# Early dot products of a product-key expert layer: from 64, 32 and 32 beside three stages to 96, 32 and none

## The reference, cut to what matters

```python
gates   = sigmoid(gate_logits + b_gate)            # gate_logits = x @ w_in[:, gate columns]
widened = einsum('bsgw,gwd->bsgd', branches, w_branch)
mix     = sum_g(gates * widened) @ w_out
h       = LN(ALPHA * x + mix)
# PEER, for blocks of 128 tokens; it, gt: 128 expert numbers and gates of each token
q    = h @ w_peer_q                                # scores, top-k -> it, gt
act  = gelu(einsum('td,ted->te', xt, u_tab[it]))   # 128 dot products of length 1024 per token
out  = einsum('te,ted->td', gt * act, v_tab[it])
```

## Time and profile before

| | |
|---|---|
| time of three runs, median | 4244.49 us (4243.42 to 4244.56) |
| the profiled execution's own time | 4240.24 us |
| its span, first to last instruction | 4238.4 us |
| busy share of PE, DVE, ACT, POOL | 87%, 64%, 32%, 37% |
| HBM traffic over the span | 267 GB/s |

### The profile page before, as it was taken

How to read it: one execution, slowest core, us unless ns; L and a number is a source line. 1 busy time by engine, 2 the same in 40 slices (tenths; PEclk the granted TensorE clock), 3 DMA queues, 4 the chain that set the end, 5 groups by cost and what they waited for, 6 DMA issues and landing times.

```text
span 4238.4 us, 46211 instructions
## 1 busy us (share of the span) xinstructions
PE 3702.3 (87%) x14431; PEld 2456.2 (58%) x14431; DVE 2717.4 (64%) x5493; ACT 1369.5 (32%) x2741; POOL 1555.7 (37%) x1317
## 2 busy tenths in 40 slices
PE   7999989799888798586437889799799999999998
PEld 5777867678777677475114445354354544545763
DVE  1444443316776766649799988988886867842550
ACT  1444443233434433126024042150240413314540
POOL 2555534230000177465455344443454544520000
PEclk8999999899999899897769999899899999999999
DMA  7667623355444377688989999999999999973557
GB/s 242 198 202 228 205 68 93 94 178 163 139 135 146 88 240 245 228 303 302 374 333 408 383 375 376 347 404 368 354 400 398 406 403 387 395 307 128 184 196 271
DMA packets 505249, 1133.37 MB, mean 267 GB/s; under 512 B 37932, under 2 KB 250076, under 8 KB 504832
## 3 DMA queue, kind: packets, MB, share of 16 engines
q1 hardware_dynamic: 336512, 570.42, 39.1%
q0 software_dynamic: 147456, 536.94, 33.3%
q10 hardware_dynamic: 21120, 24.12, 1.6%
HBM read 1044.28 MB, written 89.41 MB: 267 GB/s over the span
## 4 chain that ended last, share of the span: by engine, by line
PE 33%; DVE 14%; DMA 5%; issue 2%; ACT 1%; POOL 0%; DVEq 0%; ACTq 0%
PE ps L1262 26%; DVE u_ring L2209 6%; DMA u_ring<-in_peer_u,pidx 4%; PE ps L1248 4%; PE ps L1295 2%; DMA v_ring<-in_peer_v 1%; DVE split_v L2259 1%; ACT split_v L1673 1%; DVE hot L2201 1%; DVE hot L2202 1%; PE h_up L1237 0%; DVE pick_own L1847 0%; DVE pick_own L1852 0%; DVE got_own L1855 0%; DVE inds_own L1798 0%
## 5 line engine op out<-in xcount | busy, mean ns | idle before, releaser
L1262 PE MATMUL ps<-v_ring,table 128*128 128x512 f32 x3584 | 1594.3, 596 | 21.3 <-DMA v_ring<-in_peer_v 20.0
L895 POOL DMA_INDIRECT u_ring<-in_peer_u,pidx x896 | 862.6, 963 | 1011.5 <-DVE coefe L2209 940.3
L2209 DVE CUSTOM_DVE_ANT_0 u_ring<-u_ring,h_up 128x1024 f32<-128x1024 f32 x896 | 1060.1, 1217 | 157.9 <-DMA u_ring<-in_peer_u,pidx 148.2
L1262 PEld LDWEIGHTS ps<-v_ring,table 128*128 128x128 f32 x3584 | 664.3, 191 | 778.7 <-issue 725.2
L844 POOL TENSOR_TENSOR w_lo<-w_raw,w_hi 128x1024 fp32r<-128x1024 f32 x200 | 443.7, 2224 | 881.2 <-ACT w_hi L1368 875.9
L954 PE MATMUL ps<-x_hi,w_hi 128*128 128x512 f32 x1280 | 521.7, 408 | 61.5 <-ACT w_hi L1368 52.8
L957 PE MATMUL ps<-x_lo,w_hi 128*128 128x512 f32 x1280 | 508.4, 397 | 0.0
L1248 PEld LDWEIGHTS ps<-hot,hot 128*128 128x128 f32 x2048 | 282.5, 204 | 184.9 <-issue 103.6
L1641 ACT ACTIVATE table<-ps 128x512 f32<-128x512 f32 (+3 forms) x256 | 229.3, 896 | 431.4 <-PE ps L1248 431.4
L1629 ACT ACTIVATE hot<-hot,by_slot 128x128 f32<-128x128 f32 x1024 | 321.3, 388 | 107.6 <-DVE hot L2201 104.1
L1248 PE MATMUL ps<-hot,hot 128*128 128x128 f32 x2048 | 294.7, 290 | 61.1 <-DVE hot L2202 37.5
(11 more groups left out here) (294 smaller groups left out, 4226.0 us busy)
## 6 DMA issues: line engine op xcount, KB each, us to landing
v_ring<-in_peer_v SPq DMA_DIRECT2D x576, 512.0 KB, 6.8
w_raw<-in_w_in SPq DMA_DIRECT2D x104, 512.0 KB, 5.4
wh_d<-w_hi SPq DMA_DIRECT2D x56, 512.0 KB, 2.7
wl_d<-w_lo SPq DMA_DIRECT2D x56, 512.0 KB, 4.2
w_hi<-wh_d SPq DMA_DIRECT2D x56, 512.0 KB, 3.6
w_lo<-wl_d SPq DMA_DIRECT2D x56, 512.0 KB, 3.7
w_raw<-in_w_peer_q SPq DMA_DIRECT2D x32, 512.0 KB, 4.5
u_ring<-in_peer_u,pidx POOLq DMA_INDIRECT x896, 9.3
```

Source lines behind the costliest of these rows:

```text
L895: pool.indirect_dma_start(out=u_ring[:, slot_of(n, k), :], out_offset=None, in_=u_tab, in_offset=bass.IndirectOffsetOnAxis(ap=pidx[n % 2][ ...
L1262: last = pe.matmul(ps[2 * (n % 2) + c][:, :], table[:, row_of(n, i1), :], v_ring[:, j % V_TILES, HALF * c:HALF * c + HALF], start=(n == p ...
L2209: dve.tensor_tensor_reduce(out=u_ring[:, slot_of(n, k), :], in0=u_ring[:, slot_of(n, k), :], in1=h1_up[:, :, :].rearrange("p c n -> p (c n)"),
```

## The change

96 of block 0's slots are worked beside the gated stage (12 in each of 8 iterations), 32 beside the output projection as before, and none beside the query projection. `icole` and `dotse` get a third place, because an iteration of the gated stage now has three groups of four slots.

```diff
-E_MID, E_OUT, E_PQ = 8, 8, 8
+E_MID, E_OUT = 12, 8
 G_OUT = E_MID * (D // P) // E_ROWS
-G_PQ = G_OUT + E_OUT * (D // P // 2) // E_ROWS
+assert E_MID * (D // P) + E_OUT * (D // P // 2) == SLOTS
...
-        icole = at("icole", [P, 2, E_ROWS], U32)
-        dotse = at("dotse", [P, 2, E_ROWS])
+        icole = at("icole", [P, 3, E_ROWS], U32)
+        dotse = at("dotse", [P, 3, E_ROWS])
...
 # u_rows (POOL) and e_rows (DVE), both:
-                    s, r, g = k % E_ROWS, k // E_ROWS % 2, group + k // E_ROWS
+                    s, r, g = k % E_ROWS, k // E_ROWS % 3, group + k // E_ROWS
...
 # POOL, query projection
                         split_lo_only(t % 2, t0 + T_PQ // 2 + 2 * e + t // 2)
-                        if hf == 1:
-                            u_rows(E_PQ * t // 4, E_PQ * (t + 1) // 4, G_PQ + E_PQ // E_ROWS * e, E_ROWS * G_PQ + E_PQ * e)
...
 # DVE, gated stage, before product b, and after the third
-                            e_rows(2 * b, 2 * b + 2, E_MID // E_ROWS * j, E_MID * j)
+                            e_rows(E_MID * b // 4, E_MID * (b + 1) // 4, E_MID // E_ROWS * j, E_MID * j)
...
-                        e_rows(6, 8, E_MID // E_ROWS * j, E_MID * j)
+                        e_rows(3 * E_MID // 4, E_MID, E_MID // E_ROWS * j, E_MID * j)
...
 # DVE, query projection
                 if hf == 1:
-                    with dve.Fori(0, PH // 2) as e:
-                        e_rows(0, E_PQ, G_PQ + E_PQ // E_ROWS * e, E_ROWS * G_PQ + E_PQ * e)
                     e_gates()
```

## The result

| | before | after |
|---|---|---|
| median of six runs of each, us | 4243.32 (4236.09 to 4244.56) | 4255.7 (4248.56 to 4260.47) |
| ratio, 95% interval | | 1.0034 (1.0023 to 1.0046) |
| the profiled execution, us (span) | 4240.24 (4238.4) | 4255.91 (4254.1) |

The change makes the kernel slower by 0.34%, 14 us (10 to 20), which is more than the 0.2% that counts as no change. 4257 us had been forecast against a median of 4244.49.

What follows compares the result with a forecast made beforehand. The prediction took POOL's queue to pace the gated stage after the change, at 28.5 to 29.7 us an iteration. Gated stage +19.1 and query projection -6.8 gave +12.3 us on the 4244.49 median: 4257 us, range 4246 to 4269.

Steps and rivals of the forecast that it cites:

- POOL's work: Gated stage: four more gathers and one more copy of numbers raise POOL's iteration from 22.75 to 28.7 us.
- Waits on the ring: Gated stage: POOL's gathers wait for dot products to free ring places, 0 to 1.4 us an iteration, taken as 0.3.
- DMA neither: Gated stage: DMA is no bound, 8.65 MB in 29 us being 298 GB/s, under the output projection's 320.
- almost no wait for ACT's w_hi: Gated stage, expected sign: POOL starts w_lo every 28.5 to 29.7 us per iteration, hardly waiting for w_hi.
- Length of the stage: Gated stage grows by +19.1 us: first iteration +2.1, next six +13.4, last +3.6.
- Output projection: Output projection keeps its 32 slots and order, so 0 change, with POOL's 8.03 us a tile as cover.
- Query projection: Query projection: -4.4 us from first to last result, gelu 2.35 us earlier behind it, together -6.8 us.
- Sum: Whole kernel: +19.1 - 6.8 = +12.3 us, 4257 us against the median of 4244.49, slower by 0.29%.
- POOL has room after all: Gated stage, POOL's queue between two w_lo: added gather and its copy cost under 1.0 us; 4240 us, chance 0.10.
- The ring holds POOL: Gated stage: both order-bound waits bite with landings at 6.5 us, period 30.7 us; 4268 us, chance 0.18.
- POOL paces but less of it counts: Gated stage: first iteration absorbs its added work, tail grows 1.5 us, pace is 28.0 us; 4247 us, chance 0.17.

Runs made afterwards that it cites:

- half rows: Changed kernel with gathers of 2 KB rows instead of 4 KB, same number of requests, upper half of each ring place zero: 4245.87 us, ratio 1.0008.
- no copies: Changed kernel with POOL's loops written out and gathers taking numbers straight from pidxe, without copying them into icole: 4259.62 us, ratio 1.0042.

## Why the prediction was right, and where it was not

The direction was right, POOL's price and the gain too. The total was right partly by luck: two terms were too small, and the expert phase covered for them in the profiles. Step by step:

- **POOL's work, 28.7 us an iteration.** Measured 28.45, and 28.87 where nothing else held the stage (half rows). Right. It passed the 26.5 us of an iteration before, and the change loses by that.
- **Waits on the ring, 0.3 us.** Of the 28.5 us before the 72 gathers 3.6 are put down to dot products: four times 0.81 us and once 0.30, which stand before such gathers anyway. The ring cost about nothing, and it is not what made the period 29.7.
- **"DMA neither".** This is the step that failed, together with "almost no wait for ACT's w_hi". It weighed bytes against throughput (298 GB/s under 320) and left out the way to w_hi: landing, table load, rounding. Taking work off POOL (no copies) left the iteration at 30.1; taking the table loads away brought it to 28.63. So w_hi comes late by 1.2 us an iteration, at the first tile and in some iterations at the third; at the other tiles POOL's queue sets the time, as forecast. At the first tile the wait ends with landing and table load. At the third it ends with PE, whose clock the prediction had weighed only against the whole iteration (27.8 us under 29), and the sigmoid's table load.
- **Length of the stage, +19.1 us.** Measured, first w_lo to last instruction of DVE (1720.77): 250.5 against 225.4 us, +25.1. The parts: first iteration +2.4 (+2.1 forecast), the six +17.5 (+13.4), the last +5.2 (+3.6), where the third product waits for dot product 8 until 1712.86. The term was 6 us too small.
- **Output projection, 0.** From the first w_lo to the last sum 78.6 against 76.7 us, +2.0. This is the change's. In the traces with the same copies and 4 KB rows the eight w_lo start over 63.1, 62.9 and 62.3 us with 96 slots in the gated stage, and over 60.8, 60.6 and 60.7 with 64. The difference stands at one place, before the 114th gather of block 0. On POOL's timeline, the changed kernel and then the one before:

```profile
1765.82 0.94 POOL L866 DMA_INDIRECT e_ring<-in_peer_u,icole  x1 [3.06 <-DVE dotse L1883]
...
1852.71 0.95 POOL L866 DMA_INDIRECT e_ring<-in_peer_u,icole  x1 [2.33 <-DVE dotse L1885]
```

  Every trace in which 128 gathers run early has a pause of 1.6 to 3.4 us before this one, whatever stage it falls in; with half rows it is 2.33 us with no wait on anything that the profile shows. Before the change gather 114 fell in the query projection. Now it falls in the output projection, and the w_lo behind it starts 10.8 us after the one before it, where that was 8.2. What makes the pause is open.
- **Query projection, -6.8 us.** -4.4 and -2.3: right, twice (the changed kernel and the run that only drops the slots).
- **Sum.** At the gelu of block 0 the changed kernel is 19.6 us behind, not 12.3. The expert phase gave 3.9 us back in this pair of profiles (2335.1 us from the gelu to the end of the span, 2339.0 before); over all ten profiles it lies between 2334.1 and 2340.1 us, and I see no tie to the edits, so I take it for scatter. The ratio says +14 us, 10 to 20. That 4257 came so close to 4255.7 is luck: the gated stage was 6 us and the output projection 2 us longer than forecast, and part of that did not reach the total.
- **Rivals.** POOL has room after all: refuted by the half rows, where 28.87 us held with POOL hardly waiting. The ring holds POOL: not in the gated stage of the changed kernel, by the 3.6 us above. POOL paces but less of it counts: no, more did.

## What to carry to other kernels

Work moved beside a busy stage has to be paid in every queue that it uses: count the issuing engine's queue per iteration against the pace, and then follow the way to each weight tile again, with the landing time that the added transfers will make, the table loads on it, and the granted clock after a wait. A throughput under the limit says nothing of that. Where removing one limit gives nothing, look for a second within a microsecond of it and remove both in one run; and look at table loads in loops, which a written-out loop did away with for 27 us here.

## What the runs showed of the hardware that I had not expected

A gather takes its row numbers straight from a column of the number tile; no copy of its own is needed when the column is fixed in the program. ACT's copy and sigmoid ran on one table throughout the stage, so the two loads an iteration (1.28 us each) came from the loop and not from the functions. And POOL paused 1.6 to 3.4 us before the 114th gather in nine traces of nine, in six of them beside the output projection and in three beside the query projection.
